# Transposing token tiles by block loads, and streaming sample states past 32 query columns

## The reference, cut to what matters

```
S_n = gamma * S_{n-1} + k_n^T v_n ;  o_n = q_n S_n
o   = o_n / sqrt(mean(o_n^2) + eps)
```

## Time and profile before

| | |
|---|---|
| median of 3 runs | 1140.71 us (1139.22 to 1141.26) |
| profiled execution, its own time | 1140.91 us |
| profiled execution, span from first to last instruction | 1139.1 us |
| PE busy | 1125.9 us, 99% |
| DVE / POOL / ACT busy | 68% / 48% / 38% |
| mean DMA rate | 129 GB/s |

### The profile page before, as it was taken

How to read it: one execution, slowest core, us unless ns; L and a number is a source line. 1 busy time by engine, 2 the same in 40 slices (tenths; PEclk the granted TensorE clock), 3 DMA queues, 4 the chain that set the end, 5 groups by cost and what they waited for, 6 DMA issues and landing times. The chain is left out here.

```text
span 1139.1 us, 22001 instructions
## 1 busy us (share of the span) xinstructions
PE 1125.9 (99%) x8411; PEld 1108.5 (97%) x8411; DVE 775.7 (68%) x1153; ACT 433.2 (38%) x877; POOL 550.3 (48%) x535
## 2 busy tenths in 40 slices
PE   8999999999999999999999999999999999999996
PEld 7889999999999999999999999999999999999996
DVE  4356556556465675789777776777877777877856
ACT  6322422313224442643333333335552443544414
POOL 0144233253150431044242322322999899999992
PEclk9999999999999999999999999999999999999999
DMA  6432331331411232254435344437962544464314
GB/s 206 136 104 84 95 109 55 107 102 48 121 58 58 59 121 82 75 177 149 150 124 179 118 149 149 135 136 262 330 195 76 172 150 136 144 187 149 94 39 149
DMA packets 162521, 147.21 MB, mean 129 GB/s; under 512 B 8029, under 2 KB 124997, under 8 KB 162431
## 3 DMA queue, kind: packets, MB, share of 16 engines
q1 hardware_dynamic: 157335, 142.79, 39.2%
q10 hardware_dynamic: 5096, 3.20, 0.9%
HBM read 101.77 MB, written 44.20 MB: 128 GB/s over the span
## 5 line engine op out<-in xcount | busy, mean ns | idle before, releaser
L1977 PE MATMUL pair<-m_hi,dn_hi 128*128 128x258 f32 (+2 forms) x896 | 255.6, 285 | 0.7 <-DVE a L1737 0.3
L1977 PE MATMUL pair<-b_hi,up_hi 128*128 128x258 f32 x896 | 253.7, 283 | 0.0
L1978 PE MATMUL pair<-b_lo,up_hi 128*128 128x258 f32 x896 | 253.6, 283 | 0.0
L1978 PE MATMUL pair<-m_lo,dn_hi 128*128 128x258 f32 (+2 forms) x896 | 253.5, 283 | 0.0
L1979 PE MATMUL pair<-m_hi,dn_lo 128*128 128x258 f32 (+2 forms) x896 | 253.3, 283 | 0.0
L1979 PE MATMUL pair<-b_hi,up_lo 128*128 128x258 f32 x896 | 252.3, 282 | 0.0
L1769 PE MATMUL pair<-x_hi,w_both 128*128 128x344 f32 (+2 forms) x576 | 188.3, 327 | 0.1
L1771 PE MATMUL pair<-x_hi,w_both 128*128 128x344 f32 (+2 forms) x576 | 184.5, 320 | 0.0
L1770 PE MATMUL pair<-x_lo,w_both 128*128 128x344 f32 (+2 forms) x576 | 184.1, 320 | 0.0
L1737 DVE TENSOR_TENSOR hid<-pair,hid 128x516 f32<-128x516 f32 (+2 forms) x194 | 124.7, 643 | 77.1 <-PE pair L1979 75.0
L1977 PEld LDWEIGHTS pair<-m_hi,dn_hi 128*128 128x128 f32 x896 | 168.9, 188 | 2.3 <-issue 1.2
(11 more groups left out here) (214 smaller groups left out, 2065.9 us busy)
## 6 DMA issues: line engine op xcount, KB each, us to landing
m_raw<-m_dram SPq DMA_DIRECT2D x56, 516.0 KB, 4.9
m_dram<-hid SPq DMA_DIRECT2D x64, 258.0 KB, 3.7
up_raw<-w_up_dram SPq DMA_DIRECT2D x32, 512.0 KB, 4.9
dn_raw<-w_down_dram SPq DMA_DIRECT2D x128, 128.0 KB, 2.4
w_raw<-w_in_dram SPq DMA_DIRECT2D x27, 512.0 KB, 3.6
m_dram<-hid SPq DMA_DIRECT2D x16, 774.0 KB, 3.9
h_dram<-hid SPq DMA_DIRECT2D x8, 516.0 KB, 3.1
h_in<-h_dram SPq DMA_DIRECT2D x16, 258.0 KB, 6.1
```

The costliest lines, as they stand in the source:

```text
L1977: m_.matmul(to, shs[k], mhs[k], start=STARTS[i] and k == 0, stop=False, skip_group_check=more)
L1978: m_.matmul(to, shs[k], mls[k], start=False, stop=False, skip_group_check=more)
```

## The change

It has two parts.

**Token tiles.** Tiles 2 to 7 (`BLK`) are no longer transposed by PE. SP loads each of them a second time, in four DMAs, so that every 32 x 32 block lies in its place (`load_blocks`, into `x_blk`, two slots; runs of 32 values, 128 bytes). DVE transposes within the blocks (`x_turn`), into `hid`, which lies where `x_lo` does. ACT's `x_high` and DVE's `x_low` take their source from there, as one instruction each of 1024 elements instead of two of 512 from PSUM. `x_raw` is still loaded, for the squares. `x_turn(i + 1)` stands at the end of DVE's step `i`.

**Sample products.** A window of 32 query columns, of which the last eight are the samples', becomes the weights, and two samples' states (256 columns) move past it; four such products go to four groups of 32 output partitions of `KT_B`. DVE at `j` = 13, behind `low`, keeps each sample's own row with the masks in `pick` (two instructions, into `o_ext`). PE in the middle of `j` = 13 waits for that and multiplies `o_ext` by `fold`, which puts the eight outputs in `SMP_B` as before. ACT reads them at `j` = 13 instead of 12, and their norm at 14 instead of 13. `fold` and `pick` are made of the identity at the start. Semaphore counts elsewhere move by constants.

```diff
+BLK = range(2, XT - 1)
+TURN0 = len(BLK)
+MOVED0 = 64 * len(BLK) // 2
...
+        x_blk = [at(f"x_blk{i}", [KT, 4, SQ], F32, t + 3 * W4 + XT * P * 4 + 4096 * i) for i in range(2)]
...
+        fold, pick = small[:, 88:88 + SAMPLES], small[:, 66:68]
+        o_ext = at("o_ext", [P], F32, r1)
...
         def _(sp):
+            def load_blocks(i):
+
+                if i >= BLK[2]:
+                    sp.wait_ge(turned, i - BLK[2] + 1)
+                rows = xp[P * i:P * i + P, :].rearrange("(j b) (k q a) -> q b k j a", b=SQ, q=4, a=SQ)
+                for q in range(4):
+                    sp.dma_start(x_blk[i % 2][SQ * q:SQ * q + SQ, :, :, :], rows[q]).then_inc((sq_moved, kB_moved)[i % 2], 16)
+
             def load_x(i):
                 if i >= 3:
 
-                    sp.wait_ge(xlo_done, 2 * (i - 2))
+                    if i - 3 < BLK[0]:
+                        sp.wait_ge(xlo_done, 2 * (i - 2))
                     sp.wait_ge(ssqx_done, i - 2)
...
             load_x(1)
+            load_blocks(2)
+            load_blocks(3)
             load_x(2)
             for i in range(3, XT):
                 load_x(i)
+                if i + 1 in BLK:
+                    load_blocks(i + 1)
...
             def x_high(i, halves=(0, 1)):
 
                 c0, c1 = tok(i)
+                if i in BLK:
+                    act.wait_ge(turned, i - BLK[0] + 1)
+                    s.activation(x_hi[:, :, c0:c1], hid[:, :, c0:c1], ACT.Copy).then_inc(xhi_done, 2)
+                    return
...
-                        if j == 12:
-
-                            act.wait_ge(smp_done, 2 * h + 1)
+                        if j == 13:
+
+                            act.wait_ge(smp_done, 3 * h + 2)
                             s.activation(o_smp[:, :], SMP_B[:, 0:SAMPLES], ACT.Copy)
                             s.activation(sq_smp[:, :], SMP_B[:, 0:SAMPLES], ACT.Square).then_inc(smp_read, 1)
+                        if j == 12:
 
                             s.activation(std_o[:, 0:CHUNKS], ms_o[:, 0:CHUNKS], ACT.Sqrt, scale=1.0 / DK, bias=eps).then_inc(std_ready, 1)
...
-                        if j == 13:
-                            act.wait_ge(smp_done, 2 * h + 2)
+                        if j == 14:
+                            act.wait_ge(smp_done, 3 * h + 3)
                             s.activation(std_smp[:, :], SMP_B[:, SAMPLES:2 * SAMPLES], ACT.Sqrt, scale=1.0 / DK, bias=eps).then_inc(smp_read, 1)
...
             dve.wait_ge(ident_in, 16)
+            for g in range(4):
+                c0 = SQ * g + SQ - SAMPLES
+                rows, some = ident[:, c0:c0 + SAMPLES], ident[:, c0 + 2 * g:c0 + 2 * g + 2]
+                if g == 0:
+                    d.tensor_copy(fold, rows)
+                    d.tensor_copy(pick, some).then_inc(const_set, 1)
+                else:
+                    d.tensor_tensor(fold, fold, rows, ALU.add)
+                    d.tensor_tensor(pick, pick, some, ALU.add).then_inc(const_set, 1)
+                dve.wait_ge(const_set, 4 + g)
+
             def x_low(i, halves=(0, 1)):
 
                 c0, c1 = tok(i)
+                if i in BLK:
+                    dve.wait_ge(xhi_done, 2 * i + 2)
+                    d.tensor_tensor(x_lo[:, :, c0:c1], hid[:, :, c0:c1], x_hi[:, :, c0:c1], ALU.subtract).then_inc(xlo_done, 2)
+                    return
...
+
+            def x_turn(i):
+
+                c0, c1 = tok(i)
+                dve.wait_ge((sq_moved, kB_moved)[i % 2], 64 * ((i - BLK[0]) // 2 + 1))
+                d.transpose(hid[:, :, c0:c1].rearrange("p k (j b) -> p k j b", b=SQ), x_blk[i % 2][:, :, :, :]).then_inc(turned, 1)
...
                 if i >= 1:
                     row_rms(i - 1)
+                if i + 1 in BLK:
+                    x_turn(i + 1)
...
                         if j == 13:
 
+                            dve.wait_ge(smp_done, 3 * h + 1)
+                            mine(d.tensor_scalar(o_ext[:, :], KT_B[:, 0:P], pick[:, 0:1], None, ALU.mult))
+                            d.scalar_tensor_tensor(out=o_ext[:, :], in0=KT_B[:, P:2 * P], scalar=pick[:, 1:2], in1=o_ext[:, :], op0=ALU.mult, op1=ALU.add).then_inc(masked, 1)
                             dve.wait_ge(std_ready, h + 1)
...
                 v_rows(i)
-                if i + 2 < XT:
+                if i + 2 < XT and i + 2 not in BLK:
                     transposes(i + 2)
...
+                        if j == 13:
+                            def middle():
+                                pe.wait_ge(masked, 9 * h + 9)
+                                m_.matmul(SMP_B[:, 0:SAMPLES], o_ext[:, :], fold, start=True, stop=True).then_inc(smp_done, 1)
                         three(MAIN[t][:, 0:a1 - a0], w_pairs(n % 2, x_hi, x_lo, a0, a1), middle=middle).then_inc(main_done, 1)
...
                             pe.wait_ge(rot_added, 6 * h + 6)
-                            for b in range(SAMPLES):
-                                ins = m_.matmul(SMP_B[:, b:b + 1], state[:, b, :], q_rot[:, PROMPT + b:PROMPT + b + 1], start=True, stop=True)
+                            for g in range(4):
+                                ins = m_.matmul(KT_B[SQ * g:SQ * g + SQ, 0:2 * P], q_rot[:, COLS - SQ:COLS], state[:, 2 * g:2 * g + 2, :].rearrange("p b e -> p (b e)"), start=True, stop=True)
                             ins.then_inc(smp_done, 1)
```

More of the change, by code:

```diff
@@ L501, in turn_first @@
             def turn_first(h):
-                sp.wait_ge(turned, 3 * h + 1)
+                sp.wait_ge(turned, TURN0 + 3 * h + 1)
                 sp.dma_start(kA_dram, kA_sq[:, :]).then_inc(sq_moved, 16)
             def turn_rest(h):
-                sp.wait_ge(sq_moved, 176 * h + 16)
+                sp.wait_ge(sq_moved, MOVED0 + 176 * h + 16)
                 sp.dma_start(k_meta[0:META, :].rearrange("r (b s) -> r b s", s=SQ),
@@ L512, in turn_rest @@
                     sp.dma_start(kA_sq[SQ * j:SQ * j + SQ, SQ:SQ + CH].rearrange("r (b x) -> r b x", b=4), kA_dram[:, SQ + P * j:SQ + P * j + P].rearrange("(b r) x -> r b x", b=4)).then_inc(sq_moved, 16)
-                sp.wait_ge(turned, 3 * h + 2)
+                sp.wait_ge(turned, TURN0 + 3 * h + 2)
                 sp.dma_start(kB_dram, kB_sq[:, :]).then_inc(kB_moved, 16)
-                sp.wait_ge(kB_moved, 80 * h + 16)
+                sp.wait_ge(kB_moved, MOVED0 + 80 * h + 16)
                 for j in range(4):
@@ L519, in turn_o @@
             def turn_o(h):
-                sp.wait_ge(turned, 3 * h + 3)
+                sp.wait_ge(turned, TURN0 + 3 * h + 3)
                 sp.dma_start(o_dram, u_n[:, 0:CHUNKS * P]).then_inc(sq_moved, 16)
-                sp.wait_ge(sq_moved, 176 * h + 112)
+                sp.wait_ge(sq_moved, MOVED0 + 176 * h + 112)
                 for j in range(4):
@@ L884, in x_high @@
                 c0, c1 = tok(i)
+                if i in BLK:
+                    act.wait_ge(turned, i - BLK[0] + 1)
+                    s.activation(x_hi[:, :, c0:c1], hid[:, :, c0:c1], ACT.Copy).then_inc(xhi_done, 2)
+                    return
                 for hf in halves:
-                    act.wait_ge(xT_done, 2 * i + hf + 1)
+                    act.wait_ge(xT_done, 2 * min(i, BLK[0]) + hf + 1)
                     src = XT_B[i % 2][hf][:, :].rearrange("p (k c) -> p k c", c=P)[:, :, 0:rows_of(i)]
@@ L950, in retention @@
                     if step < 0:
-                        wait_alone(act, sq_moved, 176 * h + 96)
+                        wait_alone(act, sq_moved, MOVED0 + 176 * h + 96)
                         s.activation(k_meta[0:META, :], k_meta[0:META, :], ACT.Copy,
@@ L954, in retention @@
                     else:
-                        wait_alone(act, kB_moved, 80 * h + 80)
+                        wait_alone(act, kB_moved, MOVED0 + 80 * h + 80)
                     s.activation(k_tok[:, c0:c0 + 4, :].rearrange("p c (b s) -> p b c s", s=SQ), src.rearrange("p (b c s) -> p b c s", b=4, s=SQ), ACT.Copy,
@@ L1299, in _ @@
             dve.wait_ge(rope_ready, 1)
-            OWN = 5
+            OWN = 5 + 1
             def retention(h, step):
@@ L1438, in head @@
                 if not last:
-                    wait_alone(dve, sq_moved, 176 * h + 176)
+                    wait_alone(dve, sq_moved, MOVED0 + 176 * h + 176)
                     yr = y_raw[:, bass.ds(4 + h, 1), META:PROMPT].rearrange("p o (c b s) -> p (o c) b s", b=4, s=SQ)
@@ L1870, in retention @@
                     vc = v[:, c, bass.ds(h * P, P)]
-                    pe.wait_ge(masked, CHUNKS * h + c + 1)
+                    pe.wait_ge(masked, 9 * h + c + 1)
                     pe.wait_ge(S_ready, 9 * h + c + 1)
```

## The result

The changed kernel takes **1142.96 us** (median of 11 runs, 1141.43 to 1143.74), the kernel before 1140.76 (11 runs, 1139.22 to 1142.39). The ratio is 1.0019, 95% interval 1.0010 to 1.0028: slower by 2.2 us, just beyond no change. The forecast was 1139.7, with 1134.5 to 1147.0 as its range. The profiled execution took 1143.32 us, with a span of 1141.5.

A forecast was written before the change was run, and what follows sets the result against it. PE was taken to bound the kernel, busy for 1125.9 of 1139.1 us. 1140.9 - 5.2 (token tiles) + 4.2 (heads) = 1139.9, with the median 0.2 lower: 1139.7 us, range 1134.5 to 1147.

The forecast's parts named there:

- Token tiles, 5.2 us saved: Token-tile stage: PE loses six groups of eight transposes, five saving 0.88 us each and the first some 0.75.
- The transfers: Token-tile stage: block DMAs at 8 ns a packet stay hidden; up to 16 ns hidden, 19.5 ns gives the gain back.
- Landing more than 6 us ahead: Token-tile stage, sign of being right: the profile after shows block DMAs landing more than 6 us ahead.
- Rival (a): Token-tile stage: small packets are dear and PE waits for `x_blk`; at 24.2 ns a packet 1152.1 us; chance 0.23.
- Sample products: Heads: the products' 1.70 us on PE become four products taking 0.43 to 1.72 us, plus 0.2 for `fold`.
- p: Heads: PE time of the four sample products, 0.43 us if column groups work side by side, 1.72 one after another.
- rival (c): Heads: the column groups don't overlap, products take 1.72 us, still under the wait: the same 1139.7 us; part of the forecast.
- The wait for `o_ext`: Middle of `j` = 13 in each head: PE waits 0.9 to 2.2 us for DVE, which does `low` first.
- Rival (b): Heads: no new wait, as `low` takes 1.22 us; 1132.3 us with groups side by side, 1136.4 otherwise; chance 0.13.
- What a head loses, 1.15 us: Looped heads: L1914 starts at 129.5 instead of 128.37; three heads lose 1.15 us each, the last 0.7, together 4.2.
- The failed step: Heads, behind the wait for `o_ext`: 0.2 us for `fold` and 12 x 0.16 for the second half of `j` = 13.
- A change of less than 0.2%: Whole kernel: a change under 2.3 us, about what measurement can't tell from none; chance 0.49, faster 0.21, slower 0.30.

The follow-up runs named there:

- run 1: Changed kernel with only the token-tile part, the sample products, their waits and ACT's places as before: 1135.37 us, ratio 0.9952 to the kernel before.
- run 3: Changed kernel, both parts, with DVE making `o_ext` right behind its read of group `j` = 12, ahead of `low`: 1132.51 us, ratio 0.9928.
- run 7: Changed kernel's token-tile part alone, each block DMA cut in two, with 64-byte runs and twice as many packets: 1150.37 us, ratio 1.0093.
- run 8: Changed kernel with `o_ext` made ahead of `low`, and all four sample products in one group of 32 output partitions: 1137.54 us.
- Runs 4 and 9: Changed kernel with nine (4) or four (9) unread products of ones ahead of PE's wait for `o_ext`: 1141.32 and 1140.80 us.
- run 6: Kernel before, with one wait added: PE waits in the middle of `j` = 13 until DVE has normed `o_tok`: 1156.44 us, ratio 1.0151.

## Why the prediction was wrong, point by point

**Token tiles, 5.2 us saved: right.** 5.03 in run 1, 4.67 in the changed kernel, 5.23 in run 3. Most periods are 5.57 to 5.63 us, as forecast; the first is 5.80 and one is 5.88.

**The transfers: the right side, for a wrong reason.** I took 8 ns a packet from a sliver of the earlier trace rows; it is 15, just under the 16 from which the gain begins to go. That sum gave the 16 engines 16 x 0.4 = 6.4 us, but the window's DMA share is 1.23, so its packets stand in the trace with 7.9 us, and its 108 packets of 128 bytes with 13.0 ns each. "Landing more than 6 us ahead" did not come true: DVE's transpose of tile 4 begins at 29.79, the moment its blocks have landed, 3.8 us before PE wants them. Rival (a) was nearer than 0.23 says, and run 7 shows it in full at twice the packets. The Trainium skill, "DMA: Bandwidth & Descriptors", Specifications, asks for 512 bytes for the full rate, and says that the engine reads, modifies and writes below that. The rates agree in direction (128 bytes in 15.2 ns on 16 engines is 135 GB/s, against the 338 of the earlier trace rows), but not in the size that I read out of it: the packet is not as long as one of 512 bytes. Whether the engine reads, modifies and writes, no run here shows.

**Sample products: right.** p came out at 0.57 plus 0.09 around it, inside 0.43 to 1.72 and near its lower end; rival (c) fell by run 8. The Trainium skill, "TensorEngine Tiling (Array Packing)", Key Properties, has tiles of the array work independently and a change of mode drain it: 0.57 against 1.84 us shows the first, and the step of 0.25 in place of 0.16 from the last ordinary matmul to the first product would fit the second.

**The wait for `o_ext`: right in place, cause and length.** 0.9 to 2.2 us were forecast, and 2.11, 1.89, 1.88 and 1.31 came, behind a `low` of 3.10 (2.79 in the last head). Rival (b) did not come about by itself; run 3 makes it, at 1132.5, where it gave 1132.3.

**What a head loses, 1.15 us: 1.37 where the clock stays up.** `o_ext` ends 4.56 us behind the start of the products (203.52 + 0.35 - 199.31), with 4.53 forecast; most of the rest is PE getting going again behind the wait, for which the sum has no term: the second head is 79.39 - 77.25 = 2.14 us longer than one of run 3, and its gap is 1.89, so 0.25 us come on top of the gap. For three heads that is 0.7 us too little, and in the first `o_ext` came another 0.2 later. The last head lost 0.68, with 0.7 forecast.

**The failed step: the wait was priced at its length, at full clock.** The sum has "0.2 for `fold`, 12 x 0.16 for the second half" behind the wait. In two of four heads the clock then fell to 0.50; in the first, the last five of those 12 matmuls and the first five of the next group ran at distances of 0.29. The profile puts that at 1.54 + 1.55 = 3.1 us, and it stands nowhere in the working. Runs 4 and 9, which leave the wait and take idle time away, give 2.0 and 1.9 us back, each against the kernel before beside it. That is less than 3.1, because the other executions have fewer falls than the profiled one. Each has its mean granted clock on record: 0.9957 on average for the changed kernel (0.995 to 0.997), 0.9978 and 0.9977 for runs 4 and 9, 0.9979 for the kernel before beside them. One fall of 3.4 us at half the clock takes 0.0015 from that mean, so there are some 1.4 falls in an execution, an estimate, worth 2.2 us.

**The sum again:** -4.67 + 3 x 1.37 + 0.22 + 0.68 + 3.1 = +3.4 at the end of the heads, as measured, instead of -1.0. Then the MLP gave 1.2 us back, which lies within what that stretch varies by from profile to profile. A change of less than 0.2% had the largest chance, 0.49. The measured 0.19% lies just inside that, but its interval leaves no change out, and a small gain was forecast where a small loss came. Without the clock it would have been no change, by runs 4 and 9, and still not the forecast gain.

## What to carry to other kernels

A wait on the bounding engine costs its length, a quarter of a microsecond to get going again here, and, from some length on, what follows it at half clock: when a change adds one, look for how long the engine will stand idle, and first for a place to make its input earlier. Here two short instructions ahead of a 3 us one turned 2.2 us lost into 8.6 gained. Transfers in very small pieces are to be priced by the packet, from the trace's own busy share, before they are called hidden.

## What the runs showed of the hardware

**The granted clock after an idle stretch.** Over all profiles here: behind gaps of PE of 2.11, 2.22, 2.33, 2.71, 2.90, 2.91 and 2.91 us it fell each time; behind 1.75, 1.76, 1.76, 1.88 and 1.89 us three times in five; behind the other ten gaps in the heads and ahead of run 7's block tiles, of 0.39 to 1.52 us, never; nor behind the 0.73 us ahead of the last transposes, which all eleven profiles have. One fall costs 1.5 to 1.6 us in the heads (1.3 in the third of run 6, where part of it passed while PE was idle), and it need not stand at the gap: it came 1.4 us after PE was busy again in the changed kernel (122.98, 124.35), 0.5 us before that in the third head of run 6, and 1.9 us after in run 7. What decides in the middle group, where 1.76 fell and 1.75 did not, stays open.

**Packets.** From DRAM, at 95% busy engines, the traces have 14.9 ns for 128 bytes and 10.9 ns for 64; by the rate in the earlier trace rows it is 24.2 for 512.

**Issuing a DMA can take SP long.** The 24 block issues of the changed kernel took 0.58 us at least, 0.68 in the middle and 4.58 at most, while the transfers were behind. That SP was held up by the transfers in front of it is inferred from this alone; no run varies it. All that PE lost by these transfers is the 0.2 us ahead of tile 4.

**Column groups.** Four products of 128 rows by 32 columns, with 256 moving columns each, take 0.57 us in four groups of output partitions and 1.84 in one (run 8).
